# A fused transformer kernel on one NeuronCore: factors of two norms applied behind the products, the per-layer projection ahead of its gate, the result in three parts

## The reference

```python
x = x + merged @ w_out[i]
gate, up = jnp.split(rms_norm_2(x, g_ffn[i]) @ w_ffn_in[i], 2, axis=-1)
x = x + (jax.nn.silu(gate) * up) @ w_ffn_out[i]
ple_gate = jax.nn.sigmoid(rms_norm_2(x, g_ple[i]) @ w_ple_gate[i])
x = x + ple_gate * (p[i] @ w_ple_proj[i])
```

## Time and profile before

| | |
|---|---|
| median of 3 runs | 1797.06 us (1794.71 to 1799.57) |
| the profiled execution's own time | 1795.95 us |
| its span in the trace | 1794.6 us |
| PE busy | 1613.6 us |
| DVE busy | 962.2 us |
| ACT busy | 722.7 us |

### The profile page before, as it was taken

The page is one execution under the profiler, slowest core; times in us unless marked ns, Lnnn a source line. Parts: engine busy times, 40 slices in busy tenths (PEclk is TensorE's granted clock), DMA queues, the critical chain, the costliest instruction groups (busy, mean ns, idle before and its releaser), DMA issues.

```text
span 1794.6 us, 22518 instructions
## 1 busy us (share of the span) xinstructions
PE 1613.6 (90%) x9150; PEld 1319.4 (74%) x9150; DVE 962.2 (54%) x1655; ACT 722.7 (40%) x1222; POOL 9.4 (1%) x21
## 2 busy tenths in 40 slices
PE   5799897998899999969887989989999998899997
PEld 1377674675488888737676879977878778899987
DVE  3742664548652333366574775657644446666545
ACT  4532343225432222444244444446534343544433
POOL 0000000000000000000000000000000000000000
PEclk9899997999999999979988989999988899999998
DMA  8521110124623222212121335534431113455542
GB/s 316 161 83 59 52 67 24 36 91 137 212 94 106 98 91 94 83 41 93 56 79 67 135 123 194 185 133 145 151 117 60 48 60 118 141 187 180 187 152 71
DMA packets 57783, 203.03 MB, mean 113 GB/s; under 512 B 6224, under 2 KB 9424, under 8 KB 57552
## 3 DMA queue, kind: packets, MB, share of 16 engines
q1 hardware_dynamic: 53472, 191.91, 32.1%
q0 software_dynamic: 1552, 5.94, 1.0%
q10 hardware_dynamic: 2656, 3.74, 0.6%
HBM read 200.52 MB, written 1.05 MB: 112 GB/s over the span
## 4 chain that ended last, share of the span: by engine, by line
PE 77%; DVE 14%; ACT 6%; issue 2%; DMA 1%; ACTq 1%; DVEq 0%
PE gemm_bank L334 15%; PE gemm_bank L336 14%; PE gemm_bank L335 14%; PE misc_bank L334 6%; PE misc_bank L336 6%; PE misc_bank L335 6%; DVE wlo L1195 3%; PE misc_bank L453 2%; PE misc_bank L670 2%; ACT whi L813 1%; DMA raw<-in_stream 1%; PE misc_bank L592 1%; PE misc_bank L585 1%; PE misc_bank L683 1%; PE misc_bank L540 1%
## 5 line engine op out<-in xcount | busy, mean ns | idle before, releaser
L1195 DVE TENSOR_TENSOR wlo<-raw,whi 128x1024 fp32r<-128x1024 f32 x364 | 439.3, 1223 | 241.5 <-ACT whi L813 239.8
L334 PE MATMUL gemm_bank<-hhi,wlo 128*128 128x256 f32 (+1 forms) x1328 | 447.9, 337 | 40.5 <-DVE hlo L1491 10.9
L335 PE MATMUL gemm_bank<-hlo,whi 128*128 128x256 f32 (+1 forms) x1328 | 427.7, 322 | 0.0
L336 PE MATMUL gemm_bank<-hhi,whi 128*128 128x256 f32 (+1 forms) x1328 | 427.4, 322 | 0.0
L813 ACT ACTIVATE whi<-raw 128x1024 fp32r<-128x1024 f32 x364 | 375.3, 1051 | 104.9 <-DMA raw<-in_stream 37.2
L334 PEld LDWEIGHTS gemm_bank<-hhi,wlo 128*128 128x128 f32 x1328 | 264.1, 199 | 76.3 <-issue 40.3
L335 PEld LDWEIGHTS gemm_bank<-hlo,whi 128*128 128x128 f32 x1328 | 264.5, 199 | 17.0 <-issue 2.2
L336 PEld LDWEIGHTS gemm_bank<-hhi,whi 128*128 128x128 f32 x1328 | 263.1, 198 | 16.4
L334 PE MATMUL misc_bank<-hhi,wlo 128*128 128x256 f32 (+1 forms) x560 | 180.6, 322 | 5.0 <-DVE hlo L1504 4.4
L335 PE MATMUL misc_bank<-hlo,whi 128*128 128x256 f32 (+1 forms) x560 | 179.6, 321 | 0.0
L336 PE MATMUL misc_bank<-hhi,whi 128*128 128x256 f32 (+1 forms) x560 | 179.5, 321 | 0.0
(11 more groups left out here) (308 smaller groups left out, 2141.2 us busy)
## 6 DMA issues: line engine op xcount, KB each, us to landing
raw<-in_stream SPq DMA_DIRECT2D x364, 512.0 KB, 3.5
const_b<-in_const_b POOLq DMA_DIRECT2D x1, 1100.0 KB, 9.3
x<-in_x ACTq DMA_DIRECT2D x1, 1024.0 KB, 16.5
x<-in_ctx ACTq DMA_DIRECT2D x1, 1024.0 KB, 18.9
y<-in_hy_decay POOLq DMA_DIRECT2D x2, 512.0 KB, 8.8
arena<-in_gm_ws POOLq DMA_DIRECT2D x2, 512.0 KB, 6.2
out<-x SPq DMA_DIRECT2D x2, 512.0 KB, 2.9
y<-in_hy_w POOLq DMA_DIRECT2D x2, 256.0 KB, 7.3
```

The costliest lines, as they stand in the source:

```text
L334: mm(out, w_lo, r_hi, start=first, stop=False)
L335: mm(out, w_hi, r_lo, start=False, stop=False)
L336: return mm(out, w_hi, r_hi, start=False, stop=last)
L1195: dve.tensor_tensor(self.wlo[:, t % SPLIT, :], self.raw[:, t % RAW, :], self.whi[:, t % SPLIT, :].bitcast(F32), ALU.subtract).then_inc(*se ...
```

## The change

The factor r of the norm is the same for all features of a token, so it can be multiplied in behind the product. The changed kernel does this in both norms:

- The halves `hhi` and `hlo` are made of x * g, without r. For `g_ffn` this happens tile by tile in `wout2` (ACT L922, DVE `dve_half`), in the second half of the buffers' columns; for `g_ple` block by block behind each sum into x.
- In the feed-forward DVE multiplies the gate product by r before the tanh (L1290, out of PSUM into `tmp`), and the product of both by r squared (L1297) before it is split. r squared is one further step. ACT now takes the tanh from `tmp` (L928).
- In `pgate` DVE multiplies the product by r (L1305), ACT takes the tanh of that (L935), and DVE finishes the block before (`dve_out`).
- The sums of squares get PSUM banks of their own (`sum_bank`), so that products can go on meanwhile.
- Both `pproj` tiles stand ahead of `pgate` in the stream and on PE, with the results in the two halves of the M banks; the first waits, block by block, until DVE has read the bank. The sums of squares stand between them in groups of three and four, the last behind the first `pgate` tile.
- The order of the blocks in the last sum (`DORDER`) is computed, and the split of the per-layer input moves ahead of the down products' results.
- The result is stored in three parts, of four, three and one block.

The core of the diff:

```diff
+        up, gate = self.tiles[self.first["ffu", 2]].use, self.tiles[self.first["pgate", 2]].use
+        self.sum_bank = {"g_ffn": self.M[(up + 2) % 4], "g_ple": self.G[(gate + 3) % 4]}
+        last = (gate + 3) % 4
+        self.DORDER = [last, 4, 5, 6, 7] + [o for o in range(4) if o != last]
...
+        self.pe_tiles(1)
         self.pe_sum("g_ffn", KT - 1, TOK)
-        self.pe_tiles(2 * FT + FT)
-        for i in range(KT):
+        self.pe_tiles(2 * FT - 1 + FT)
+        self.pe_tiles(1)
+        for i in range(3):
             self.pe_sum("g_ple", i, TOK)
-        pe.wait_ge(*self.at("dacc", 7))
-        self.pe_tiles(KT)
-        self.pe_tiles(2)
+        self.pe_tiles(1)
+        for i in range(3, 7):
+            self.pe_sum("g_ple", i, TOK)
+        for o in range(4):
+            pe.wait_ge(*self.at("dacc", o))
+        self.pe_tiles(1)
+        self.pe_sum("g_ple", 7, TOK)
+        self.pe_tiles(KT - 1)
...
+        elif kind == "ffg":
+            if j == 0:
+                self.act_root("g_ffn", TOK)
+            th = self.tmp[:, T.use % 2, 0:TOK]
+            act.wait_ge(*self.at("ffn_g", j))
+            act.activation(th, th, ACT.Tanh, scale=0.5).then_inc(*self.mark("act_ffn", "ffn_tanh", j))
         elif kind == "ffu":
-            act.activation(th, self.M[T.use % 4][:, 0:TOK], ACT.Tanh, scale=0.5).then_inc(*self.mark("act_ffn", "ffn_tanh", j))
             act.wait_ge(*self.at("ffn_mul", j))
...
         elif kind == "wout2":
+            if j:
+                self.dve_half("g_ffn", j - 1, TOK)
+        elif kind == "ffg":
+            if j == 0:
+                self.dve_rstd("g_ffn", TOK)
+                self.own(dve.tensor_tensor(self.tmp[:, 2, TOK:ALL], self.tmp[:, 2, 0:TOK], self.tmp[:, 2, 0:TOK], ALU.mult))
+            dve.wait_ge(*self.at("used", T.t))
+            dve.tensor_tensor(self.tmp[:, T.use % 2, 0:TOK], self.M[T.use % 4][:, 0:TOK], self.tmp[:, 2, 0:TOK], ALU.mult).then_inc(*self.mark("dve_ffn", "ffn_g", j))
         elif kind == "ffu":
-            dve.tensor_tensor(th, th, b[:, 0:TOK], ALU.mult).then_inc(*self.mark("dve_ffn", "ffn_mul", j))
+            self.own(dve.tensor_tensor(th, th, b[:, 0:TOK], ALU.mult))
+            dve.tensor_tensor(th, th, self.tmp[:, 2, TOK:ALL], ALU.mult).then_inc(*self.mark("dve_ffn", "ffn_mul", j))
...
         v.wait_ge(*self.at("used", self.dve_done - 1))
+        self.dve_tiles(2)
         for i, o in enumerate(self.DORDER):
-            v.tensor_tensor(self.x[:, o, 0:TOK], self.x[:, o, 0:TOK], self.out_banks[o][:, 0:TOK], ALU.add).then_inc(*self.mark("dve_x", "dacc", i))
+            v.tensor_tensor(self.x[:, o, 0:TOK], self.x[:, o, 0:TOK], self.out_banks[o][:, 0:TOK], ALU.add).then_inc(*self.mark("dve_x", "dacc", o))
+            if i >= 1:
+                self.dve_half("g_ple", self.DORDER[i - 1], 0)
+        self.dve_half("g_ple", self.DORDER[-1], 0)
         self.dve_tiles(KT)
-        self.dve_tiles(2)
+        self.dve_out(KT - 1)
...
+        for g, (a, b) in enumerate(((0, 4), (4, 7), (7, 8))):
+            sp.wait_ge(*self.at("out", b - 1))
+            sp.dma_start(self.out[:, a:b, :], self.x[:, a:b, 0:TOK]).then_inc(*self.landing(f"out{g}"))
```

More of the change, by code:

```diff
@@ L163, in plan @@
         add("down", 2, f, TOK, 0)
+    for g in range(2):
+        add("pproj", 2, g, TOK, 0)
     for o in range(KT):
         add("pgate", 2, o, TOK, 1)
-    for g in range(2):
-        add("pproj", 2, g, TOK, 0)
     return tiles, extra
@@ L173 @@
     SPREAD = (4, 5, 10, 11, 12, 13)
-    DORDER = (4, 0, 1, 2, 3, 5, 6, 7)
     def __init__(self, nc, ins, out):
@@ L344, in pe_feature @@
     def pe_feature(self, T, bank, hi, lo, begun=None, col=0):
-        for k in range(KT):
+        at = TOK if T.kind in ("ffg", "ffu") else 0
+        tk = slice(at, at + T.n)
+        for i in range(KT):
+            k = i
             if begun:
+                k = self.DORDER[i] if T.kind == "pgate" else i
                 self.pe.wait_ge(*self.at(*begun, k))
             c = slice(col + k * P, col + (k + 1) * P)
-            m = self.three(bank[:, 0:T.n], hi[:, c], lo[:, c], self.hhi[:, k, 0:T.n], self.hlo[:, k, 0:T.n], k == 0, k == KT - 1)
+            m = self.three(bank[:, 0:T.n], hi[:, c], lo[:, c], self.hhi[:, k, tk], self.hlo[:, k, tk], i == 0, i == KT - 1)
         return m
@@ L375, in pe_tile @@
             begun = {"k": ("h", T.l), "wout": ("merged", T.l), "zc": ("hn", "g_mix"), "wout2": ("merged", 2), "pgate": ("hn", "g_ple")}.get(kind)
+            if kind == "pgate" and j == 3:
+                pe.wait_ge(*self.at("rstd", "g_ple"))
             m = self.pe_feature(T, self.pe_bank(T.use), hi, lo, begun if lead else None)
@@ L452, in pe_sum @@
         self.pe.wait_ge(*self.at("sq", stage, k))
-        self.pe.matmul(self.M[0][:, 0:n], self.c["mean_all"], self.tmp[:, k % 2, 0:n], start=first, stop=last).then_inc(*self.mark("pe_sum", "summed", stage, k))
+        self.pe.matmul(self.sum_bank.get(stage, self.M[0])[:, 0:n], self.c["mean_all"], self.tmp[:, k % 2, 0:n], start=first, stop=last).then_inc(*self.mark("pe_sum", "summed", stage, k))
     def pe_filter(self, l):
@@ L803, in act_root @@
         self.act.wait_ge(*self.at("summed", stage, KT - 1))
-        self.act.activation(self.tmp[:, 2, 0:n], self.M[0][:, 0:n], ACT.Sqrt, bias=self.c["eps"]).then_inc(*self.mark("act_root", "root", stage))
+        self.act.activation(self.tmp[:, 2, 0:n], self.sum_bank.get(stage, self.M[0])[:, 0:n], ACT.Sqrt, bias=self.c["eps"]).then_inc(*self.mark("act_root", "root", stage))
     def act_hi(self):
@@ L1268, in dve_tile, with dve_out, dve_half @@
             self.also("ffn_lo", j)
-        elif kind == "pproj":
+        elif kind == "pgate":
+            if j == 0:
+                self.dve_rstd("g_ple", TOK)
             dve.wait_ge(*self.at("used", T.t))
-            for o in range(4):
-                k = 4 * j + o
-                yk, xk = self.y[:, k, 0:TOK], self.x[:, k, 0:TOK]
-                dve.wait_ge(*self.at("evac", self.tiles[self.first["pgate", 2] + k].use))
-                dve.scalar_tensor_tensor(yk, yk, 1.0, self.M[o][:, 0:TOK], ALU.add, ALU.mult).then_inc(*self.mark("dve_ple", "ple_mul", k))
-                dve.wait_ge(*self.at("ple_mul", k))
-                dve.scalar_tensor_tensor(xk, yk, 0.5, xk, ALU.mult, ALU.add).then_inc(*self.mark("dve_out", "out", k))
+            dve.tensor_tensor(self.y[:, j, 0:TOK], b[:, 0:TOK], self.tmp[:, 2, 0:TOK], ALU.mult).then_inc(*self.mark("dve_evac", "evac", T.use))
+            if j:
+                self.dve_out(j - 1)
+    def dve_out(self, k):
+        yk, xk = self.y[:, k, 0:TOK], self.x[:, k, 0:TOK]
+        self.dve.wait_ge(*self.at("ple_tanh", k))
+        self.own(self.dve.scalar_tensor_tensor(yk, yk, 1.0, self.M[k % 4][:, (k // 4) * TOK:(k // 4 + 1) * TOK], ALU.add, ALU.mult))
+        self.dve.scalar_tensor_tensor(xk, yk, 0.5, xk, ALU.mult, ALU.add).then_inc(*self.mark("dve_out", "out", k))
+    def dve_half(self, gain, k, at):
+        self.dve.wait_ge(*self.at("hn_hi", gain, k))
+        self.dve.scalar_tensor_tensor(self.hlo[:, k, at:at + TOK], self.x[:, k, 0:TOK], self.c[gain][:, k:k + 1], self.hhi[:, k, at:at + TOK].bitcast(F32), ALU.mult, ALU.subtract).then_inc(*self.mark("dve_half", "hn", gain, k))
     def dve_sine(self, arg, k, big=False, shift=0.0):
```

50 lines of the change are left out of this document (24 added, 26 removed).

## The result

The changed kernel takes 1814.26 us, median of 4 runs (1812.23 to 1815.64), against 1797.95 for the kernel before in the same batch (4 runs, 1794.71 to 1799.57): a ratio of 1.0092, 95% interval 1.0077 to 1.0107, so slower by 16.3 us where 12.8 were forecast. The profiled execution has 1815.64 us and a span of 1814.3. Against the 1809 that the prediction named as the time itself, 1814.26 is 5.3 us more: 3.5 is the change, 0.9 the kernel before (1797.95 in this batch, 1797.06 when the prediction was made), and 0.9 a slip in its last sum, since 1808.8 and the 1.1 that it adds make 1809.9.

The account below looks back on a forecast made before the run. PE bounds the feed-forward before, a loop through DVE and ACT after. Later down products +19.6, clock +1.9 and tail -8.7 make +12.8 on 1795.95, 1808.8, stated as 1809 us; likeliest 1803 to 1816, 8 in 10 1799 to 1819.

Parts of the forecast that it names:

- The round, R = 6.90: Feed-forward: DVE and ACT alternate on one loop of 6.90 us per round, over PE's 5.76; bounds 6.6 to 7.1.
- The clock in the feed-forward: Feed-forward, rival: PE's pauses make the clock fall; 1879 us if in all 22 rounds, 1825 if in five; chance 5%.
- The row of `up`: Earlier `up` stage: PE pauses 1.0 us per round with the clock at 1.00, so such pauses were priced at nothing.
- The pause and the clock ahead of the down products: End of the feed-forward: PE pauses some 6 us, then the clock falls, costing +1.9 us; bounds 0 and 2.4.
- `wout2`: Stage ahead of the feed-forward: making `hhi` and `hlo` there costs nothing, hidden under PE's 3.3 us per tile.
- uncovered: `wout2`: cost of the added half steps if PE did not hide them, 2.8 us; not in the sum.
- The tail: From the end of the down products to the kernel's end: 44.2 us instead of 52.9, -8.7; bounds -12 and -3.

Follow-up runs that it names:

- e1: Changed kernel with only the order moved: both `whi` and both `wlo` of a feed-forward round together at the gate tile; 1792.93 us, 0.998 of the kernel before.
- e2: Changed kernel without the multiplication by r squared in the feed-forward, one DVE step less per round; 1806.3 us, 1.0042 of the kernel before.
- e4: Changed kernel with ACT's high-half Copy in `wout2` moved behind the next tile's `whi`; 1810.6 us, 1.0078 of the kernel before.
- e5: Changed kernel with the tail reordered: first `pgate` `whi` and `wlo` later, four buffers for the Squares instead of two; 1809.03 us, 1.0067 of the kernel before.
- e8: Changed kernel with splits together, `wout2` Copy behind `whi`, tail reordered, r squared applied behind the down products; 1781.66 us, 0.9907 of the kernel before.

## Why the prediction was right, and where it was short

- **The round, R = 6.90.** Right to 0.01 us (6.903), hop by hop. From the last sum into x, the first full round was to start 11.03 us later and did (1546.71 to 1557.74); the down products 156.6 us later, and did. Part of the 11.03 is luck: I let the root wait for PE's last sum, 3.6 us behind the last sum into x. PE had that sum done at about 1549.6, and what held the root was ACT's own list, which the prediction did not count there: Square, Copy, `whi` and a load of the function's tables of 1.28 us (1549.00), so that the root started at 1550.29, 3.58 behind 1546.71. From the root on, the hops are those of the prediction. `wlo` stands in pairs 2.99 and 3.90 apart (1558.81, 1561.80, 1565.70), as foretold. e1 and e2 show that it is a loop and not a load: moving steps gave 21 us, removing one gave a whole hop per round.
- **The clock in the feed-forward.** It stayed at 1.00 over 138 us with a wait of PE in each round. By the Trainium skill, "TensorE: Matmul & The Clock Gate", section "A second HAM failure mode: psum-queue depth-cycling", these short idles could have made it swing; here they did not. The row of `up` that I leaned on holds three rounds of 6.83 and not four, and the 1.02 us in it is the weight loads' wait; PE's own there is 0.79 to 0.85. PE's busy share was 89% where I had said 84%: the modelled end of a matmul (0.28 long, 0.12 apart) covers part of each wait, so 0.77 us of idle is shown (row at 1642.89) for a loss of 1.14.
- **The pause and the clock ahead of the down products.** Forecast 6 us and +1.9; measured 6.23 and +2.2. The mechanism held, the size was 0.3 off: the row that I took it from gives 2.3 (21 matmuls in 4.8 us instead of 2.5), and I had put 1.9 without saying why. The six pauses of 4.45 to 6.25 us in the table cost 1.6 to 2.5.
- **`wout2`.** This is the step that failed. The prediction put it so: "Cost nothing: PE's tile takes 24 x 0.12 + 0.42 = 3.3 us with its sum". I compared each engine's own work with PE's 3.3, the very reading that I had rejected for the feed-forward one paragraph earlier. Both engines have slack there, but the loop through them had at most 0.25 us against PE, and the Copy takes 0.39. In most of the stage it had none: the sums were behind PE and catching up, so nothing covered the Copy. It costs 2.30 us, near the 2.8 that I named for "uncovered" but did not take into the sum. e4 shows it by moving that one instruction.
- **The tail.** Right in its steps, 0.9 us short in size: -7.8 instead of -8.7. Half a us is lost by the third Square already, because `pproj`'s first 24 matmuls took 4.66 us, most of them at the low pace, where I had allowed 4.3 (a slip: at the 0.21 that I named, 24 matmuls are 5.0 us; the first six at full pace made up a part of it). The rest is spread over what follows: `pproj`'s second tile took 3.06 instead of 2.9 (1778.42 to 1781.48), the four sums 2.15 instead of 2.0, the first `pgate` tile 3.06 instead of 2.9, and from there to the reciprocal 3.2 instead of 3.1. e5 shows that the two `wlo` ahead of the first sum, the low clock and the held Squares together were worth 4.6 us.
- **Start of the kernel.** The +3.3 us of the profiled span ahead of `wout2` is no effect of the change: the same instructions end there anywhere within 5.2 us. One sees it only by measuring from an instant close to the edit, or from the medians of the runs.

## What to carry to other kernels

Where two in-order engines hand work back and forth, add up the hops around the closed loop, not the busy time of each: a loop can bind with both engines half idle, and it must be summed in every stage that the edit touches. A loop that is shorter than PE's round has slack only once it has caught up with PE: in `wout2` that was so from the sixth of seven distances on, and up to there an added step cost its whole length. Steps that only prepare later tiles cost the loop one pass over both engines if they are split up between the dependent steps (21 us here), so keep them together, and put a step whose result is needed later behind the one that the loop waits for. A factor that is common to all features of a token can be moved once more, out of the repeated round to the place where it is applied least often.

## What the runs showed of the hardware

- The granted clock can fall in the middle of a burst: behind a pause of 3.5 us, six matmuls ran 0.12 us apart before the pace became 0.21. I had expected the low pace from the first matmul, as in the down products (0.35, then 0.22).
- A pause of 1.82 us ahead of the down products and one of 1.21 ahead of `pproj` left the clock at 1.00; in e8 one of 2.2 us ahead of `pproj` was followed by 0.68 over 5.4 us. These stand behind different work, so they give no rule for the length alone.
- The same instructions, up to the first sum into x of `wout2`, ended anywhere within 5.2 us in ten executions, while the stretches behind it repeated to 0.03 us wherever the clock did not fall and their own code was the same.
- Ahead of the root ACT loaded the tables of its function for 1.28 us (1549.00 in the changed kernel), and the root started right behind it, at 1550.29. The load ahead of the first tanh (1550.79, 1.28 us) cost nothing, since the tanh waited for DVE until 1553.51.
